# Turned softmax rows and values of a decoder step: stored and fetched by another engine, and past keys and values loaded at other steps

## The reference

```python
u, gp, q, k, v, ga = split_proj(h, w_in)
a = dilated_attn_prompt(q, k, v, slopes)          # softmax(q k^T + bias) v, causal
xp = xp + merge_out(pm, gp, a, ga, w_out, dtype)
k_p.append(k[:, T - keep:]); v_p.append(v[:, T - keep:])
# sample tokens: the same against cache_k_win and cache_v_win (2048 past rows, 8 sequences)
```

## Time and profile before

| | us |
|---|---|
| median of 3 runs | 821.46 (821.45 to 824.18) |
| the profiled execution's own time | 821.09 |
| its span, first to last instruction | 819.3 |
| granted TensorE clock, mean | 0.996 |

### The profile page before, as it was taken

The page is one execution under the profiler, slowest core; times in us unless marked ns, Lnnn a source line. Parts: engine busy times, 40 slices in busy tenths (PEclk is TensorE's granted clock), DMA queues, the critical chain, the costliest instruction groups (busy, mean ns, idle before and its releaser), DMA issues.

```text
span 819.3 us, 17483 instructions
## 1 busy us (share of the span) xinstructions
PE 807.1 (99%) x6625; PEld 802.6 (98%) x6625; DVE 627.4 (77%) x1347; ACT 398.9 (49%) x875; POOL 203.2 (25%) x340
## 2 busy tenths in 40 slices
PE   9999999999999999999999999999999999999995
PEld 8999999999999999999999999999999999999994
DVE  4657895897589778958885897689888886777765
ACT  4745435533554454345435533553465345555554
POOL 2103502520360045014402610450000131222220
PEclk9999999999999999999999999999999999999998
DMA  8569647856774696578558756884668567766565
GB/s 297 142 173 232 168 125 171 231 144 168 188 208 122 163 233 169 152 175 228 152 141 186 204 147 182 193 214 123 172 195 272 156 181 203 207 184 174 150 180 218
DMA packets 271499, 150.04 MB, mean 183 GB/s; under 512 B 44448, under 2 KB 261472, under 8 KB 271392
## 3 DMA queue, kind: packets, MB, share of 16 engines
q1 hardware_dynamic: 239784, 118.97, 53.7%
q0 software_dynamic: 12672, 20.59, 9.9%
q10 hardware_dynamic: 18960, 9.38, 4.0%
HBM read 119.49 MB, written 28.27 MB: 180 GB/s over the span
## 4 chain that ended last, share of the span: by engine, by line
PE 87%; DVE 6%; DMA 3%; issue 1%; ACT 1%; SPq 1%; POOL 1%; DVEq 0%; ACTq 0%
PE pj L889 64%; PE pj L1048 13%; PE ps_s L946 1%; PE ps_s L948 1%; PE ps_o L977 1%; PE ps_o L975 1%; DMA out<-arena 1%; PE ps_o L889 1%; DVE w_lo L1624 1%; PE ps_t L995 1%; PE ps_s L995 1%; PE ps_s L889 1%; PE ps_s L827 1%; DVE arena L1755 1%; DMA w_raw<-in_w_out 0%
## 5 line engine op out<-in xcount | busy, mean ns | idle before, releaser
L889 PE MATMUL pj<-mov_hi,w_hi 128*128 128x260 f32 (+1 forms) x1632 | 332.1, 285 | 0.3 <-DVE mov_lo L1645 0.3
L889 PE MATMUL pj<-mov_hi,w_lo 128*128 128x260 f32 (+1 forms) x1632 | 328.3, 283 | 0.0
L889 PE MATMUL pj<-mov_lo,w_hi 128*128 128x260 f32 (+1 forms) x1632 | 327.8, 282 | 0.0
L889 PEld LDWEIGHTS pj<-mov_hi,w_hi 128*128 128x128 f32 x1632 | 252.7, 189 | 2.1 <-issue 0.6
L889 PEld LDWEIGHTS pj<-mov_lo,w_hi 128*128 128x128 f32 x1632 | 251.4, 188 | 0.0
L889 PEld LDWEIGHTS pj<-mov_hi,w_lo 128*128 128x128 f32 x1632 | 251.4, 188 | 0.0
L1148 ACT ACTIVATE w_hi<-w_raw 128x640 fp32r<-128x640 f32 (+1 forms) x157 | 121.4, 773 | 228.5 <-PE pj L889 159.3
L1624 DVE TENSOR_TENSOR w_lo<-w_raw,w_hi 128x640 fp32r<-128x640 f32 (+1 forms) x157 | 135.5, 863 | 62.7 <-ACT w_hi L1148 62.3
L1566 POOL DMA_DIRECT2D p_scratch<-extra x168 | 104.8, 631 | 82.4 <-DVE extra L1727 79.9
L1597 POOL DMA_DIRECT2D y_scratch<-arena x56 | 37.6, 678 | 110.5 <-DVE arena L2209 81.3
L1540 POOL DMA_DIRECT2D out<-arena x8 | 4.6, 569 | 213.0 <-DMA arena<-arena 213.0
(11 more groups left out here) (275 smaller groups left out, 1295.3 us busy)
## 6 DMA issues: line engine op xcount, KB each, us to landing
w_raw<-in_w_in SPq DMA_DIRECT2D x96, 320.0 KB, 4.1
w_raw<-in_w_in SPq DMA_DIRECT2D x48, 384.0 KB, 4.5
arena<-in_cache_k_win SPq DMA_DIRECT2D x16, 384.0 KB
arena<-in_cache_v_win SPq DMA_DIRECT2D x16, 384.0 KB
p_scratch<-extra POOLq DMA_DIRECT2D x112, 48.0 KB, 3.3
w_raw<-in_w_out SPq DMA_DIRECT2D x26, 192.0 KB, 3.0
arena<-in_cache_k_win SPq DMA_DIRECT2D x8, 512.0 KB
arena<-in_cache_v_win SPq DMA_DIRECT2D x8, 512.0 KB
```

What stands on the lines that cost most here:

```text
L889: mm = pe.matmul(dst[h][:, 0:own.stop - own.start], w, m[:, k, own], start=(k == 0 and i == 0), stop=(c == 2 and k == KT - 1 and i == 2))
```

## The change

The values of pairs one to seven are no longer turned by PE. DVE turns them in 32x32 blocks at j = 9, into the buffer that the keys' turn uses too (`kv_sq`); POOL stores them straight to the output `v_win` with four DMAs, waits for these to land, and loads them back tokens by features with one DMA. Their split moves from j = 12 to j = 15. The fetches of the turned softmax rows move from ACT's queue to POOL's, at fixed places between POOL's stores. The keys' turn (j = 13) also waits until the values' stores have landed. SP loads past keys one step sooner and past values three steps sooner, and no longer stores the values, except for the last pair, which keeps the old way.

```diff
 # SP
-                    if j in (5, 6, 7):
-                        load_keys(pr, j - 5)
-                    if j in (10, 11, 12):
-                        load_values(pr, j - 10)
+                    if j in (4, 5, 6):
+                        load_keys(pr, j - 4)
+                    if j in (7, 8, 9):
+                        load_values(pr, j - 7)
-                    if j == 14:
-                        sp.wait_ge(v_nat_c, pr + 1)
+                    if j == 14 and p is FINAL:
+                        sp.wait_ge(v_nat_c, 1)
                         sp.dma_start(v_out[:, :, P * pr:P * pr + P],
...
 # PE, j == 10
-                    for t in range(QT):
-                        tr = turn(ps_m[:, P * t:P * t + P], z_v[:, P * t:P * t + P])
-                    tr.then_inc(v_nat_t, 1)
+                    if p is FINAL:
+                        for t in range(QT):
+                            tr = turn(ps_m[:, P * t:P * t + P], z_v[:, P * t:P * t + P])
+                        tr.then_inc(v_nat_t, 1)
...
 # ACT
-                for h in range(2):
-                    if p is not FINAL and p.s[h] + 5 <= j < p.s[h] + 8:
-                        load_turned(pr, h, j - p.s[h] - 5)
-                    act.wait_ge(v_nat_t, pr + 1)
-                    act.activation(v_nat, ps_m[:, :], ACT.Copy).then_inc(v_nat_c, 1)
+                    if p is FINAL:
+                        act.wait_ge(v_nat_t, pr + 1)
+                        act.activation(v_nat, ps_m[:, :], ACT.Copy).then_inc(v_nat_c, 1)
-                if j == 12:
-                    act.wait_ge(v_nat_c, pr + 1)
+                if j == (12 if p is FINAL else 15):
+                    act.wait_ge(*((v_nat_c, 1) if p is FINAL else (v_nat_in, 16 * pr + 16)))
...
 # POOL
+            def send_values(pr):
+                pool.wait_ge(v_nat_t, pr + 1)
+                for a in range(SQS):
+                    at = P * pr + SQ * a
+                    pool.dma_start(v_sq_out[:, :, at:at + SQ],
+                                   kv_sq[SQ * a:SQ * a + SQ, :].rearrange(
+                                       "p (c x) -> p c x", x=SQ)).then_inc(y_st[2], 16)
+            def load_values(pr):
+                pool.wait_ge(y_st[2], Y_ST * (pr + 1))
+                pool.dma_start(v_nat.rearrange("p (t x) -> p t x", t=QT),
+                               v_out[:, :, P * pr:P * pr + P]).then_inc(v_nat_in, 16)
...
-                send_k_row(pr)
                 if pr < SENT:
-                    for u in range(3):
-                        send_turned(pr, 0, u)
+                    send_values(pr)
+                    send_turned(pr, 0, 0)
+                    send_turned(pr, 0, 1)
+                    load_values(pr)
+                    send_k_row(pr)
+                    load_turned(pr, 0, 0)
+                    send_turned(pr, 0, 2)
+                else:
+                    send_k_row(pr)
                 if pr > 0:
                     send_split(pr - 1 + PAIRS)
+                if pr < SENT:
+                    load_turned(pr, 0, 1)
+                    load_turned(pr, 0, 2)
                 send_v_row(pr)
                 send_u(pr)
                 if pr < SENT:
                     for u in range(3):
                         send_turned(pr, 1, u)
+                    for u in range(3):
+                        load_turned(pr, 1, u)
...
 # DVE
-                if j == 12:
+                if j == (12 if p is FINAL else 15):
                     dve.wait_ge(v_hi_done, pr + 1)
...
+                if j == 9 and p is not FINAL:
+                    dve.wait_ge(tile_out, 6 * pr + 5)
+                    if pr > 0:
+                        dve.wait_ge(kv_st, KV_ST * pr)
+                    dve.transpose(kv_sq, z_v[:, 0:SEQ]).then_inc(v_nat_t, 1)
                 if j == p.kn:
...
+                    dve.wait_ge(y_st[2], Y_ST * min(pr + 1, SENT))
+                    dve.transpose(kv_sq, z_k[:, 0:SEQ]).then_inc(k_turned, 1)
```

More of the change, by code:

```diff
@@ L38 @@
 Y_ST = 16 * SQS
-KV_ST = 16 * (1 + SQS)
+KV_ST = 16 * SQS
 PARTS = P // NB
@@ L105 @@
 TURN_AT = (0, 384)
-OUT_ST = (Y_ST * 4 * SENT, Y_ST * 2 * SENT, 0)
-OUT_IN = tuple(16 * len(u) * 2 * SENT for u in UNITS)
+KV_ALL = KV_ST * PAIRS + 16
+OUT_ST = (Y_ST * 4 * SENT, Y_ST * 2 * SENT, Y_ST * SENT)
+OUT_IN = (32, 32, 32)
 C_ID, C_DIST, C_NLOG, C_SLOPE, C_SB, C_INV, C_IW, C_OWN, C_END = np.cumsum(
@@ L279, in layer_step @@
         t16 = take(16)
-        u_sq, k_sq = take(2 * SQ), take(SEQ)
+        u_sq, kv_sq = take(2 * SQ), take(SEQ)
         mix_in = [kk[:, NT * i:NT * i + NT] for i in range(5)] + [z_q]
@@ L428, in layer_step @@
         yt_done = sem("yt_done")
-        y_st, y_in = [sem(f"y_st{i}") for i in range(3)], [sem(f"y_in{i}") for i in range(3)]
+        y_st, p_in = [sem(f"y_st{i}") for i in range(3)], [sem(f"p_in{i}") for i in range(3)]
+        y_in = [mov_in[i] for i in (8, 9, 10)]
         y_added, y_squared = sem("y_added"), sem("y_squared")
@@ L772, in _ @@
                     sp.wait_ge(m_split, len(SPLIT_ORDER) + 4)
-                    sp.wait_ge(kv_st, KV_ST * PAIRS)
+                    sp.wait_ge(kv_st, KV_ALL)
                     load_res(0)
@@ L812, in _ @@
             sp.wait_ge(f_st, 16 * (2 * (len(Y_AT) - 1) + 1 + 2 * (len(ROW_AT) - 1)))
-            for s, n in ((kv_st, KV_ST // 16 * PAIRS), (kn_st, PAIRS), (vn_st, PAIRS),
+            for s, n in ((kv_st, KV_ALL // 16), (kn_st, PAIRS), (vn_st, PAIRS),
                          (us_st, SQS * PAIRS), (up_st, SQS * PAIRS), (hist_st, 1),
@@ L1032, in attention @@
                     else:
-                        pe.wait_ge(v_nat_c, PAIRS)
+                        pe.wait_ge(v_nat_c, 1)
                     pe.matmul(av_bank(pr)[:, 0:2 * NB], av, own_share, start=True,
@@ L1211, in p_hi @@
                 a.then_inc(pt_hi_done, 1)
[L1213 to L1219, removed]
-                    act.dma_start(pt_lo[:, 0:i + 1, P * i:P * i + P].bitcast(F32),
-                                 p_dram[6 * pr + 3 * h + u, at:at + n].rearrange(
-                                     "(j p) q -> p j q", p=P)).then_inc(y_in[u], 16)
             def p_hi_sent(pr, h, u):
-                act.wait_ge(y_in[u], 16 * len(UNITS[u]) * (2 * pr + h + 1))
+                act.wait_ge(p_in[u], 16 * len(UNITS[u]) * (2 * pr + h + 1))
                 if u == 0 and 2 * pr + h > 0:
@@ L1567, in send_turned, with load_turned @@
                         "p (b r) -> p b r", r=SQ)).then_inc(y_st[TURN_SLOT[u]], 16)
+            def load_turned(pr, h, u):
+                pool.wait_ge(y_st[TURN_SLOT[u]], Y_ST * (turns_sent(pr, h, u) + 1))
+                if 2 * pr + h > 0:
+                    pool.wait_ge(pv_done, 2 * pr + h)
+                for i, at in UNITS[u]:
+                    n = P * (i + 1)
+                    pool.dma_start(pt_lo[:, 0:i + 1, P * i:P * i + P].bitcast(F32),
+                                 p_dram[6 * pr + 3 * h + u, at:at + n].rearrange(
+                                     "(j p) q -> p j q", p=P)).then_inc(p_in[u], 16)
             for pr in range(PAIRS):
@@ L2030, in late @@
                         dve.wait_ge(kv_st, KV_ST * pr)
-                    dve.transpose(k_sq, z_k[:, 0:SEQ]).then_inc(k_turned, 1)
+                    dve.wait_ge(y_st[2], Y_ST * min(pr + 1, SENT))
+                    dve.transpose(kv_sq, z_k[:, 0:SEQ]).then_inc(k_turned, 1)
                 if j == p.ur:
@@ L2142, in form_sums @@
                     dve.wait_ge(form_sum, 2)
-                    dve.wait_ge(kv_st, KV_ST * PAIRS)
+                    dve.wait_ge(kv_st, KV_ALL)
                     dve.wait_ge(p_turned, 6 * PAIRS)
```

9 lines of the change are left out of this document (5 added, 4 removed).

## The result

The changed kernel takes 844.9 us (median of 4 runs, 842.24 to 847.1) against 822.76 us (4 runs, 821.45 to 824.18) beside it: 1.0246, interval 1.0211 to 1.0282. It is 2.5% slower, where I had forecast 0.4% less. (A ratio in this document is estimated from the fast runs of both kernels, so it is not quite the quotient of the two medians, here 1.027.) The profiled execution took 847.1 us, its span is 845.3 us.

A forecast was written before the change was run, and what follows sets the result against it. PE's list of products was taken to bound the kernel (busy 99%). The only nonzero term was 7 x 0.43 = 3.0 us saved: 821.46 - 3.0 = 818.4 us, 0.37% less, called the same; range 817.6 to 822.0.

The forecast's parts named there:

- The turns, 0.43 us a pair: PE, step 10: dropping four turns shortens 0.78 us between starts to 0.35, saving 0.43 us a pair, 3.0 us over seven.
- The first rival: PE: the 28 turns are worth their full 0.272 us each, 7.6 us, giving 813.8 us; chance 0.05.
- Cost: nothing: SP and DMA queues: sooner past loads only shift ACT's weight waits; cost nothing, between 0 and the second rival's price.
- The second rival: Weights come late behind six steps of past loads; PE loses 2 us a pair, +11, 832.4 us; chance 0.07.
- which comes out of the lead of 3.9 us: DVE, step 15: work behind the values' low split slips 0.76 us plus a similar wait, absorbed by a weight chunk's lead.
- PE does not feel it: Second head's rows fetched by POOL: ACT waits 1.4 us (worst 4.7), nothing (worst 3.0) off a lead of 3.9.
- POOL: right that it is no bound: POOL gets 13 issues at 0.62 us, 8.1 us a pair of some 76, on an engine busy 25%.
- the third rival: POOL's fetches, held up by DVE, come late: 1.9 us a pair, +13.3 - 3.0, 831.8 us; chance 0.06.
- I leave it there: PE's granted clock stays at 1.00, the upper level (2.4 GHz), since PE has no more idle time than before.

The follow-up runs named there:

- Run 4: The kernel before with PE's four turns of the values made twice in pairs one to seven; ratio 1.0003, pairs two to seven longer by 0.44 us each.
- run 17: The kernel before with past keys one step sooner and values by DVE and POOL in pairs two to five only, fetches on ACT, states first; 0.9957, 820.76 us.
- run 2: The kernel before with only the sooner loads (past keys at steps 4 to 6, past values at 7 to 9); PE still turns the values; 1.0107.
- run 14: The kernel before with only the past values loaded three steps sooner; 1.0396.
- run 13: The kernel before with only the past keys loaded one step sooner; 0.9971.
- run 18: The kernel before with only the past keys loaded one step sooner, measured again; 0.9961, 821.84 us against 823.76 beside it.
- run 10: The kernel before with only the values' two splits, on ACT and DVE, moved from step 12 to 15; 1.0108.
- run 5: The kernel before with only the fetches of turned softmax rows moved from ACT's list to POOL's, in the change's order; 1.0007.
- run 6: The kernel before with only the values' path changed (turned by DVE, through POOL, split at step 15); fetches on ACT, past loads at old steps; 1.0286.
- run 11: The kernel before with values by DVE and POOL, split at 15 behind the states' turns, fetches on ACT, past values loaded at steps 13 to 15; 1.0112.
- run 8: The changed kernel with the sooner past loads in pairs two to seven only; 1.0192.
- run 15: The changed kernel with past values back at their old steps, keys still sooner, and the pool states' turns ahead of the values' split on DVE; 1.0053.
- run 16: The changed kernel, past values at old steps, keys sooner, states first, fetches on ACT, pair one's values also turned by PE; 1.0002.
- run 1: The changed kernel with past keys and values loaded at their old steps (5 to 7 and 10 to 12); 1.0295, 849.36 us.
- run 3: The changed kernel with past loads at their old steps and DVE turning the pool states ahead of the values' split; 1.0162.
- run 7: The changed kernel with sooner past loads in pairs two to seven only and the pool states' turns ahead of the values' split on DVE; 1.0095.
- run 12: The kernel before with the values' split at step 15, on DVE behind the turns of the row and of the pool states; 1.0054.

## Why the prediction was wrong

- **The turns, 0.43 us a pair: right.** Run 4 gives 0.44, run 17 gives 0.43 in three of four pairs, and the third product starts 0.35 us after the states' turn (288.98 to 289.33), as worked out. The first rival (full duration) falls with it. It is the one term that I had sized, and a small one.
- **"Cost: nothing" for SP and the DMA engines: this step failed.** The sooner loads alone cost 1.07% (run 2). Of the two it is the past values that cost, 3.96% by themselves (run 14); the keys save 0.3 to 0.4% (runs 13 and 18). I had compared the DMA share of two windows, and that did not say what stands behind a late weight load. The second rival had the late weights, and its 832.4 us are near run 2's 834.0, but by luck: its 2 us in each of seven pairs fell as +10.2 us in pair one and +3.4 in pair eight, and PE waited for scores and rows, not for the weights themselves.
- **"which comes out of the lead of 3.9 us" and "PE does not feel it": this step failed too.** The leads of 3.9 to 7.3 us are those of weight chunks (and 3.9 was not the tightest of pair four: at step 2 DVE is done at 248.35 and PE comes at 251.96, 3.6 us). The scores had 1.7 us and the turned rows 0.6 us in every second pair of the kernel before, and PE's waits of pairs one to seven are nearly all for these. The slip at step 15 that I let pass costs 1.08% by itself (run 10), about half of it through the pool states' turns. I had said that they slip and that POOL's fetches move with them, but set that microsecond against the lead of a weight chunk, not of the rows that POOL carries.
- **POOL: right that it is no bound.** It is busy 32% now. An issue of a fetch takes 746 ns (median) against the 0.62 us taken, a store 633 against 617. The fetches cost nothing that run 5 can tell, 0.34% at most, and the third rival, with 13.3 us, falls. The Trainium skill's rule on GpSimd's DMAs and VectorE's port (SBUF — State Buffer, "SBUF: two separate sides") says that the former can starve while the latter runs an instruction that takes their shared port. The stores' issue times show no sign of it; whether the fetches' 572 to 774 ns hold any of it, no run here shows.
- **The clock: "I leave it there" failed.** It assumed no new idle time on PE. One stall of 3.53 us came with 6.8 us at the lower level, 2.8 us lost.
- **The parts do not add.** Loads 1.07, output 0.30, late split 1.08, fetches 0.07, turns -0.36 (3.0 of 822.8) make 2.2%; the change has 2.46, and the intervals, 0.3 to 0.4% to either side, leave room for that. But the values' path with the past values at their old steps costs 2.86% (run 6), far above 0.30 + 1.08 - 0.36 = 1.0. There POOL's load of the values lands after 5.4 to 6.8 us, in the change after 3.5 (and after 7.6 to 8.5 in run 11, with the past values still later), and weights issued at steps 12 and 13 after 7.8 and 7.5 (4.1 and 5.7 before). So the sooner loads make room for the round trip (1.0295 to 1.0192 in pairs two to seven, run 8) and lose part of that in pair one (83.64 to 93.26 us, 1.0192 to 1.0246).

What stays open: how the remaining half of the late split's price divides between ACT and DVE, how much of the weights' lateness is SP's issuing and how much the landing, why the keys are worth 1.1% in run 15 and 0.3 to 0.4% in the kernel before, and why pair seven stalls at step 15 in runs 15 and 16 where pairs three to five do not.

## What to carry to other kernels

An engine that never waits has a lead over each of its inputs, and the smallest of them is the cover, not that of the input one happens to watch: list the last producer of every operand of PE and its distance, before anything is costed at nothing. Here bulk loads that were moved on a shared queue made some of the weights issued behind them late; what that cost was decided by what stood behind those weights in the waiting engine's list, so read that list first. When a saving is small (0.43 us a pair here), try the parts one by one: here the part that was only meant to make room, the keys, was most of the gain.

## What was unexpected of the hardware

- Towards the end of a PE stall of 3.53 us the granted clock fell to 0.5 and stayed there for 6.8 us. Stalls of about 2.7 us at step 4 of pair two (runs 1, 3, 6, 7, 8, 10, 12) were each followed by 3.4 us at 0.5, worth 1.6 us more (in run 1 a stretch takes 4.00 us for 2.36 before); a stall of 3.52 us in pair four of run 14 was followed by none, so the length of the stall does not settle it.
- Weight loads of 320 to 384 KB that land in about 3.3 us in steps without past loads took up to 11.2 us in the step in which SP also issues two loads of past rows (run 14).
- Four DMAs of 16 KB that SP issues in 2.6 to 3.2 us in the kernel before took it up to 6.4 us where past values are issued just ahead of them (the change; 6.2 in run 14).
